# Seven-product feed-forward: weight slots split in the order of use, P1 copied inside PSUM, all weight sums on GpSimd

## The reference

```
def swiglu(x, w13, w2):
    a, b = jnp.split(x @ w13, 2, axis=-1)
    return (jax.nn.silu(a) * b) @ w2
h + 0.5 * gate * swiglu(modulate(rms_norm_2(h, g), shift, scale), w13, w2)
```

## Time and profile before

| | us |
|---|---|
| median of 3 runs | 4215.4 |
| profiled execution | 4207.03 |
| its span | 4205.2 |
| TensorE busy | 3955.2 (94%) |
| VectorE busy | 2774.1 (66%) |
| ScalarE busy | 1794.9 (43%) |
| GpSimd busy | 363.9 (9%) |

### The profile page before, as it was taken

One profiled execution on the slowest core, in us unless ns is written; L12 is line 12 of the kernel. 1 busy time (PEld: TensorE's weight loads), 2 busy tenths in 40 slices (PEclk: granted clock), 3 DMA queues, 4 the chain that ended last, 5 costly groups with the idle time before them and its releaser, 6 DMA issues. The chain is left out here.

```text
span 4205.2 us, 93389 instructions
## 1 busy us (share of the span) xinstructions
PE 3955.2 (94%) x40440; PEld 3503.4 (83%) x40440; DVE 2774.1 (66%) x4482; ACT 1794.9 (43%) x3112; POOL 363.9 (9%) x279
## 2 busy tenths in 40 slices
PE   6999999998999998999999999999999999989999
PEld 5777877776788887899996778999989999658998
DVE  6565666654444444788875547888778888657776
ACT  4443443332355554543443425433454334435443
POOL 0111111001000000011101210111001110120000
PEclk9999999999999999999999999999999999999999
DMA  4001000005245545111211111111111111212232
GB/s 172 19 14 28 28 28 28 28 6 200 101 171 182 180 175 207 51 63 69 71 73 61 58 36 55 61 70 71 71 51 70 71 71 61 84 58 72 103 108 81
DMA packets 99882, 337.07 MB, mean 80 GB/s; under 512 B 5009, under 2 KB 66834, under 8 KB 71826
## 3 DMA queue, kind: packets, MB, share of 16 engines
q1 hardware_dynamic: 99474, 331.09, 22.0%
HBM read 326.62 MB, written 4.46 MB: 79 GB/s over the span
## 5 line engine op out<-in xcount | busy, mean ns | idle before, releaser
L1549 PE MATMUL banks<-x_hi,w_hi 128*128 128x384 f32 (+2 forms) x1968 | 668.3, 340 | 38.8 <-DVE w_lo L1780 36.7
L1550 PE MATMUL banks<-x_lo,w_hi 128*128 128x384 f32 (+2 forms) x1968 | 661.4, 336 | 0.0
L1551 PE MATMUL banks<-x_hi,w_lo 128*128 128x384 f32 (+2 forms) x1968 | 661.2, 336 | 0.0
L1672 ACT CAST w_hi<-landing_all 128x512 fp32r<-128x512 f32 x666 | 394.3, 619 | 385.1 <-DVE landing_all L1789 156.3
L1780 DVE TENSOR_TENSOR w_lo<-landing_all,w_hi 128x512 fp32r<-128x512 f32 x666 | 456.2, 690 | 68.2 <-ACT w_hi L1672 67.8
L1549 PEld LDWEIGHTS banks<-x_hi,w_hi 128*128 128x128 f32 x1968 | 371.8, 189 | 62.9 <-issue 51.5
L1550 PEld LDWEIGHTS banks<-x_lo,w_hi 128*128 128x128 f32 x1968 | 372.1, 189 | 2.1
L1551 PEld LDWEIGHTS banks<-x_hi,w_lo 128*128 128x128 f32 x1968 | 371.7, 189 | 2.0
L1549 PE MATMUL banks<-g_hi,w_hi 128*128 128x384 f32 x840 | 282.1, 336 | 19.1 <-issue 19.1
L1831 DVE SCALAR_TENSOR_TENSOR x_res<-banks,small,x_res 128x384 f32<-128x384 f32 (+1 forms) x600 | 272.3, 490 | 29.3 <-PE banks L1551 28.0
L1550 PE MATMUL banks<-g_lo,w_hi 128*128 128x384 f32 x840 | 280.7, 334 | 0.0
(11 more groups left out here) (545 smaller groups left out, 9382.1 us busy)
## 6 DMA issues: line engine op xcount, KB each, us to landing
landing_all<-in_w SPq DMA_DIRECT2D x132, 1024.0 KB, 4.8
arena_first<-in_ada_w SPq DMA_DIRECT2D x38, 2048.0 KB, 8.7
weight_ring_first<-in_rw_pair SPq DMA_DIRECT2D x32, 512.0 KB, 5.0
landing_all<-in_w_in SPq DMA_DIRECT2D x12, 1024.0 KB, 4.8
weight_ring_first<-in_da_head SPq DMA_DIRECT2D x16, 512.0 KB, 9.6
weight_ring_first<-in_da_head SPq DMA_DIRECT2D x8, 1024.0 KB, 6.2
landing_all<-in_w_out SPq DMA_DIRECT2D x8, 1024.0 KB, 5.0
x_normed_first<-in_ada_w SPq DMA_DIRECT2D x3, 2048.0 KB, 11.1
```

The source lines that it names most:

```text
L1549: mm(o, wh, xh, start=first, stop=False, skip_group_check=onto)
L1550: mm(o, wh, xl, start=False, stop=False, skip_group_check=onto)
L1551: return mm(o, wl, xh, start=False, stop=last, skip_group_check=onto)
L1672: nc.scalar.copy(SH[:, q % RING], raw(q)).then_inc(whi.h, 1)
```

## The change

The slots are now numbered in the order in which TensorE uses them, so the ring gives out places in that order, and up to two splits per slot. The order of use is changed too: a g unit is now P1, (P4 of the unit before), P5, (P3 of the unit before), P6, P2, P7; a w unit is P1, (held), P2, (held), P5, P6, P3, P7 and holds only P4 back. ScalarE copies P1's bank into P2's bank, and P2's matmuls add onto that copy; so VectorE's addition of P2 in g units and its addition of P1 to the residual in w units go away, and SiLU reads the bank. All weight sums, also of g units, are made by GpSimd; a sum's wait is the split of the last raw quarter that it overwrites. ScalarE's cast of P5, P7, P6 or P4 waits for GpSimd's sum. The numbers X1 to X3 shrink to X2 and X3.

```
 units += [("w", 4, 0), ("w", 4, 1), ("w", 5, 0)]
+for unit in units:
+    kind, u, _ = unit
+    if unit not in sevens:
+        slots += held + [(unit, part) for part in range(4)]
+        held = []
+    elif kind == "g":
+        slots += [(unit, P1)] + held[0:1] + [(unit, P5)] + held[1:2] + [(unit, P6), (unit, P2), (unit, P7)]
+        held = [(unit, P4), (unit, P3)]
+    else:
+        slots += [(unit, P1)] + held[0:1] + [(unit, P2)] + held[1:2] + [(unit, P5), (unit, P6), (unit, P3), (unit, P7)]
+        held = [(unit, P4)]
...
-            if nxt < Q and used_up(nxt - RING) <= n + 1:
-                splits_at[-1].append(nxt)
+            while nxt < Q and used_up(nxt - RING) <= n + 1 and len(splits_at[n]) < 2:
+                splits_at[n].append(nxt)
                 nxt += 1
...
             def _(pool):
-                for q0, s in sevens.items():
-                    if slots[q0][0] == "g":
-                        continue
+                for unit, s in sevens.items():
...
+                def copy_first(q, ab=0):
+                    unit = slots[q][0]
+                    if freed[unit, 1, ab]:
+                        sig_, count = freed[unit, 1, ab]
+                        act.wait_ge(sig_.h, sig_.at(0, count))
+                    copy_product(q, bank(bank_at(unit, P2, ab)), ab)
...
             def _(dve):
                 def split(q):
...
-                    dve.wait_ge(wlo.h, wlo.at(0, q + 1))
-                    if made:
-                        dve.wait_ge(wsum.h, wsum.at(0, 4 * sevens[q0] + made))
-                    tt(out, x, y, ALU.subtract).then_inc(wsum.h, 1)
...
-                    elif u >= PLAIN and part == P2:
-                        done()
-                        dve.wait_ge(copied.h, copied.at(0, s + 1))
-                        add_bank(q, X1)
```

More of the change, by code:

```diff
@@ L1405, in ffn_sevens @@
         target = ((0, 0), (0, 0), (1, 1), (1, 1), (1, 0), (0, 1), (1, 0))
-        w_order = (P1, P2, P6, P5, P7, P3, P4)
         units = []
         for u in range(FT):
-            units.append(("g", u))
+            units.append(("g", u, 0))
             if u % 4 == 0 and 4 <= u <= 16:
[L1412 to L1415, removed]
@@ L1426, in ffn_sevens @@
[L1426 to L1438, removed]
@@ L1439, in ffn_sevens @@
[L1439 to L1442, removed]
+                units += [("w", u // 4 - 1, 0), ("w", u // 4 - 1, 1)]
+        units += [("w", 4, 0), ("w", 4, 1), ("w", 5, 0)]
+        loads = {unit: n for n, unit in enumerate(units)}
+        sevens = {unit: n for n, unit in enumerate(x for x in units if (x[1] >= PLAIN if x[0] == "g" else x[1] < 5))}
@@ L1443, in ffn_sevens @@
+        Q = len(slots)
+        slot_of = {x: q for q, x in enumerate(slots)}
+        last_slot = [max(q for q in range(Q) if slots[q][0] == unit) for unit in units]
+        used_up = lambda q: (slot_of[slots[q][0], 3] if slots[q][0][0] == "g" and slots[q][0][1] < PLAIN else q) + 1
         splits_at, nxt = [], RING
@@ L1486, in ffn_sevens, with allot @@
         sil_ready, g_ready, ghi, glo, g_sums = sig("silu_a_ready0"), sig("g_full_ready0"), sig("g_hi_ready0"), sig("g_lo_ready"), sig("g_sums_made")
[L1488 to L1499, removed]
+        banks, released, release, freed = {}, [-1] * 8, [None] * 8, {}
+        def allot(key, at, until, sig_, count):
+            b = min((n, b) for b, n in enumerate(released) if n < at)[1]
+            banks[key], freed[key] = b, release[b]
+            released[b], release[b] = until, (sig_, count)
+        for q, (unit, part) in enumerate(slots):
+            kind, u, _ = unit
+            if unit in sevens and part in (P1, P5):
+                for x, last in ((0, P4), (1, P2)) if part == P1 else ((2, P3),):
+                    for ab in range(2 if kind == "w" else 1):
+                        end = slot_of[unit, last]
+                        s = u - PLAIN
+                        use = (out_done, out_no[end, ab]) if kind == "w" else ((sil_ready, 2 * u + 2), (sil_ready, 2 * u + 1), (u_made, 2 * s + 2))[x]
+                        allot((unit, x, ab), q, end, *use)
+            elif kind == "g" and part == 0 and unit not in sevens:
                 for x in range(4):
-                    allot((q0, x), n, n + 3)
+                    allot((unit, x), q, q + 3, *((sil_ready, 2 * u + x + 1) if x < 2 else (g_ready, 2 * u + x - 1)))
             elif (kind, u, part) == ("w", 5, 0):
                 last_bank = min((max(released[b:b + 2]), b) for b in (0, 2, 4, 6))[1]
-        bank_at = lambda q, ab=0: banks[slots[q][4], bank_of[slots[q][2]], ab]
-        plain_bank = lambda u, n: banks[begin["g", u], n]
+        bank_at = lambda unit, part, ab=0: banks[unit, bank_of[part], ab]
+        plain_bank = lambda u, n: banks[("g", u, 0), n]
         out_bank = lambda n: (last_bank + 2 * n) % 8
@@ L1629, in _ @@
                 self.keep_awake(0, 7)
-                for q in order:
-                    kind, u, part, _, _ = slots[q]
+                for q, ((kind, u, _), part) in enumerate(slots):
                     if (kind, u) == ("w", 5):
@@ L1851, in after @@
                 def after(n):
-                    q = order[n]
-                    kind, u, part, _, _ = slots[q]
-                    s = 3 * (u - PLAIN)
+                    unit, part = slots[n]
+                    kind, u, _ = unit
+                    s = 2 * (u - PLAIN)
                     done = lambda: dve.wait_ge(slot_done.h, slot_done.at(0, n + 1))
```

237 lines of the change are left out of this document (115 added, 122 removed).

## The result

The changed kernel took 4192.36 us, the median of 4 runs (4184.31 to 4195.17), beside 4213.9 for the kernel before on the same chip: ratio 0.9945, 95% interval 0.9931 to 0.9958. It is faster by 21.5 us, where 40 were forecast; 4175 was predicted, in a range of 4147 to 4209.

The account below looks back on a forecast made before the run. TensorE was taken to bound the kernel, waiting 19.8 us per call before P6. Per call 19.8 - 5.0 (start) - 1.5 (conflict) = 13.3 us, 40 over three calls: 4175 us, range 4147 to 4209.

Parts of the forecast that it names:

- The waits before P6: 198 slots from g4.P1: TensorE waits 19.8 us per call for late splits of P6; earlier splits remove all of it.
- Residual waits: 198 slots: conflict between VectorE and GpSimd costs 1.5 us per call, taken near the lower bound.
- the taking of turns: VectorE instructions with two SBUF inputs and GpSimd sums exclude each other; two multiplications took 2.23 us against 1.03.
- the prediction's own signs: Right: 198 slots in 412 to 415 us; wrong: waits before P3, P7 or P4 in w units, among others.
- 14.6 us of queue: Each split is given out seven slots ahead, which evens out conflicts not lost on average; reason for 1.5 us per call.
- VectorE's 284 us without conflicts: 198 slots: VectorE busy 358 us before less 74, plus whatever its conflicts add.
- The start: From g2.P1 to g4.P1, with the ring still empty: 5.0 us lost per call, P7 of g2 some 19 us after P1.
- The second stretch of slow matmuls: Start: two idle holes now, each followed by matmuls at the lower clock; 0 to 3.1 us more, 1.5 added.
- The 0.2 us of slack before P7: After a pair of g units, once per cycle, ScalarE's queue leaves about 0.2 us before P7 is late.
- A conflict that costs nothing: Rival: start gains 0.5 us, the rest loses nothing; 20.3 us gained per call, 4154 us; chance 0.10.
- Rival 2: No change: VectorE and GpSimd fill the cycle one after the other, 91.1 us; 4222 us; chance 0.08.
- The slower one: Rival: g units' sums take 1.506 us on GpSimd and all block VectorE; cycle 94.5 us, 4270 us; chance 0.09.

Follow-up runs that it names:

- order_alone: Changed kernel with g units' weight sums on VectorE and the load that the PSUM copies removed given back to VectorE: 4201.3 us, 0.9979 of the kernel before.
- length_kept: Changed kernel with GpSimd's sums cut to 8 columns, each behind three fills of a spare tile that read nothing: 4169.3 us, 0.9907 of the kernel before.
- tiny_sums: Changed kernel with each GpSimd weight sum over 8 of 512 columns, all waits and signals kept: 4141.4 us, 0.9835 of the kernel before.
- start_on_vector: Changed kernel with the weight sums of g2 and g3 of each call made by VectorE: 4179.3 us, 0.9924 of the kernel before.

## Why the prediction was right, and where its size was off

**The waits before P6.** Right: all are gone from the 198 slots, and the pace of 411.8 us was reached where the sums cost nothing (411.98). But the prediction put all of the 19.8 us down to the order, and none of the load taken from VectorE on TensorE's path by itself. In the new order that load is on it: with the additions put back, waits of some 9.7 us a call stand in the w units (order_alone, roughly, since the load has another place there), and the order alone brings some 3. That the pace could be reached at all was luck in so far as the change also took this load away.

**Residual waits: the term that was mis-sized.** 1.5 us a call was put, 7.9 was measured (419.69 less 411.8). One place was named (P4 of wA, behind VectorE's accumulations), and so was the taking of turns; the wait before P1 of wA was not. By the prediction's own signs this part came out wrong: 412 to 415 us were to show it right, and waits before P3, P7 or P4 in w units to show it wrong. What failed is the reason for taking the low end, that 14.6 us of queue even out what is not lost on average. VectorE had 98 us free in the 198 slots, but little of it in the w units: between P1 and P4 of wA, 19.4 us, two gaps of 0.35 and 1.0 in the first four cycles. The second is not even room: the split that VectorE waits for there depends on sum 3 of wB, and the accumulations stand behind it. This chain of GpSimd, ScalarE and VectorE was followed for g units only; in w units no time was put for it, and its length makes some 2.9 of the 7.9 us (length_kept). Counted by groups over the 198 slots, after and then without the reading sums (tiny_sums):

```profile
L1783 DVE TENSOR_TENSOR w_lo<-landing_all,w_hi 128x512 fp32r<-128x512 f32 x196 | 151.3, 793 | 34.8 <-ACT w_hi L1666 34.6
L1825 DVE SCALAR_TENSOR_TENSOR x_res<-banks,small,x_res 128x384 f32<-128x384 f32 x60 | 35.1, 609 | 3.1 <-PE banks L1548 2.8
L1791 DVE TENSOR_TENSOR ffn_tiles<-ffn_tiles 128x384 f32<-128x384 f32 x38 | 24.5, 683 | 0.7
```

```profile
L1783 DVE TENSOR_TENSOR w_lo<-landing_all,w_hi 128x512 fp32r<-128x512 f32 x196 | 130.1, 685 | 32.5 <-ACT w_hi L1666 32.5
L1825 DVE SCALAR_TENSOR_TENSOR x_res<-banks,small,x_res 128x384 f32<-128x384 f32 x60 | 35.6, 613 | 5.6 <-PE banks L1548 5.6
L1791 DVE TENSOR_TENSOR ffn_tiles<-ffn_tiles 128x384 f32<-128x384 f32 x38 | 19.5, 555 | 0.7
```

Splits and gatings grew by 108 and 128 ns, accumulations out of PSUM not at all. VectorE's 284 us without conflicts came out as 285.1 (tiny_sums), and conflicts added 36.9. With GpSimd filling instead of summing, VectorE was busy for 285.8 us (length_kept). The Trainium skill (SBUF — State Buffer, "Who interferes with whom") says that a VectorE instruction with two SBUF inputs does not contend with a GpSimd instruction that only writes SBUF; length_kept agrees.

**The start.** 5.0 us lost a call was predicted, 4.4 measured; P7 of g2 came 18.3 us after P1, 19.2 were forecast. 3.7 of it is GpSimd's making of the sums (start_on_vector). The second stretch of slow matmuls was there too, from the start of P7 on, after 2.32 us of idleness; TensorE's timeline, for the earlier trace rows (granted clock over this start 0.86):

```profile
1767.53 0.69 PE L1546 MATMUL banks<-x_hi,w_hi 128*128 128x384 f32 x1 [2.32 <-ACT ffn_tiles L1704]
...
1768.33 0.52 PE L1548 MATMUL banks<-x_hi,w_lo 128*128 128x384 f32 x1
```

**The g units.** The 0.2 us of slack before P7 once in a cycle was nearly right: P7 waits there, for 0.17 us (0.5 once).

**The sum.** 11.9 (198 slots) less 4.4 (start) is 7.5 us a call, 22.6 in all, for a forecast of 40.

**The rivals.** A conflict that costs nothing was to give 4154; the run without reading or length gave 4141, since the start gains more than was counted. Rival 2, a cycle of 91.1 us, did not come: the cycle took 88.94, and of the 31.1 us of GpSimd 7.9 came on top of VectorE's 60.0. The slower one did not come either, nor its reason: undisturbed, a sum of a g unit took 1.29 us like one of a w unit. Above all sum 2, which lies beside splits, was long, 1.77 us on average in the 198 slots, in units of both kinds.

## What to carry to other kernels

Room on average says little of an engine that several others wait for in one phase: count its free time in that phase, with each instruction at the length that it has beside its neighbours, and follow the chain that each instruction at the head of its queue waits for. Moving work with two SBUF operands from VectorE to GpSimd returned only 26 of 47 us here and made its chain longer. The parts of this change that paid were the order and the additions left to PSUM. Of the placements of the sums that were tried, that of g units and the first w unit on VectorE, and of the second on GpSimd, had the lowest ratio.

## What the hardware showed beside that

ScalarE's copy from bank to bank took 0.46 us, no more than that from a bank to SBUF (0.48), which no row of before had shown; both are from one cycle of the changed kernel:

```profile
L1704 ACT COPY ffn_tiles<-banks 128x384 f32<-128x384 f32 x9 | 4.3, 480 | 7.4 <-PE banks L1548 7.4
L1704 ACT COPY banks<-banks 128x384 f32<-128x384 f32 x8 | 3.7, 464 | 5.4 <-PE banks L1548 5.4
```
